# Routing of a two-layer trunk: expert loads held behind two row gathers, token table made before the gates

## What is computed

```python
x = x + concat([y_a, y_b, y_c]) @ w_out[l]
h2 = rmsnorm(x, norm2_g[l])
x = x + hier_moe(h2, ...)      # top-1 of 4 groups, top-2 of its 4 experts
# hier_moe
gate = one_hot(g_sel) * (p_g * w_e)
for gi in range(N_GROUPS):
    a = einsum('td,edh->teh', t, w_gate[gi]); b = einsum('td,edh->teh', t, w_up[gi])
    y = y + einsum('teh,ehd->td', silu(a) * b * gate[:, gi, :, None], w_down[gi])
```

## Time and profile before

| | us |
|---|---|
| median of 3 runs | 1200.66 (1200.47, 1200.66, 1204.75) |
| the profiled execution | 1201.01 |
| its span, first to last instruction | 1199.2 |
| PE busy in the span | 1143.3 (95%) |
| DVE, ACT busy | 999.9 (83%), 739.2 (62%) |
| granted TensorE clock, mean | 0.986 |

### The profile page before, as it was taken

How to read it: one execution, slowest core, us unless ns; L and a number is a source line. 1 busy time by engine, 2 the same in 40 slices (tenths; PEclk the granted TensorE clock), 3 DMA queues, 4 the chain that set the end, 5 groups by cost and what they waited for, 6 DMA issues and landing times.

```text
span 1199.2 us, 17704 instructions
## 1 busy us (share of the span) xinstructions
PE 1143.3 (95%) x5852; PEld 914.0 (76%) x5852; DVE 999.9 (83%) x1548; ACT 739.2 (62%) x1052; POOL 117.2 (10%) x156
## 2 busy tenths in 40 slices
PE   5999998999999999999889999989999999999995
PEld 4876885688788888888778668757887888888884
DVE  4997996447799999999769889863478999999997
ACT  5234238433688888888642341682337888888884
POOL 5100000001011111110400000000000111111022
PEclk9999999999999999999999999999989999999998
DMA  9722211128999999999864122012399999999987
GB/s 301 276 97 88 77 33 50 53 88 283 326 373 394 393 391 393 393 392 380 201 205 123 53 88 88 19 36 79 118 327 332 392 393 392 392 393 391 392 284 202
DMA packets 145564, 290.35 MB, mean 242 GB/s; under 512 B 17104, under 2 KB 19216, under 8 KB 145472
## 3 DMA queue, kind: packets, MB, share of 16 engines
q1 hardware_dynamic: 130176, 237.63, 55.5%
q0 software_dynamic: 15296, 51.56, 12.9%
HBM read 263.43 MB, written 25.69 MB: 241 GB/s over the span
## 4 chain that ended last, share of the span: by engine, by line
PE 67%; DVE 7%; ACT 3%; DMA 3%; issue 2%; POOL 2%; POOLq 0%; ACTq 0%; DVEq 0%
PE ps L387 19%; PE ps L389 18%; PE ps L388 18%; DVE w_lo L379 2%; PE ps L748 2%; PE ps L606 2%; DMA arena<-y_rows,yidx 2%; POOL x_sb L578 1%; PE ps L881 1%; PE ps L867 1%; PE ps L844 1%; PE ps L767 1%; PE ps L891 1%; DVE x_sb L1394 1%; DMA y_rows<-pw 1%
## 5 line engine op out<-in xcount | busy, mean ns | idle before, releaser
L387 PE MATMUL ps<-w_hi,a_hi 128*128 128x512 f32 x960 | 380.9, 397 | 5.7 <-DVE w_lo L379 4.8
L375 ACT ACTIVATE w_hi<-raw 128x1024 fp32r<-128x1024 f32 (+1 forms) x256 | 267.5, 1053 | 183.4 <-PE ps L389 173.2
L389 PE MATMUL ps<-w_hi,a_lo 128*128 128x512 f32 x960 | 375.0, 391 | 0.0
L388 PE MATMUL ps<-w_lo,a_hi 128*128 128x512 f32 x960 | 374.7, 390 | 0.0
L379 DVE TENSOR_TENSOR w_lo<-raw,w_hi 128x1024 fp32r<-128x1024 f32 (+1 forms) x256 | 302.2, 1209 | 52.3 <-ACT w_hi L375 44.0
L379 DVE TENSOR_TENSOR w_lo<-arena,w_hi 128x1024 fp32r<-128x1024 f32 x192 | 227.9, 1222 | 9.7 <-ACT w_hi L375 1.4
L375 ACT ACTIVATE w_hi<-arena 128x1024 fp32r<-128x1024 f32 x192 | 203.6, 1063 | 44.1 <-PE ps L389 39.1
L387 PEld LDWEIGHTS ps<-w_hi,a_hi 128*128 128x128 f32 x960 | 180.7, 188 | 43.9 <-issue 4.5
L389 PEld LDWEIGHTS ps<-w_hi,a_lo 128*128 128x128 f32 x960 | 180.6, 188 | 38.3
L388 PEld LDWEIGHTS ps<-w_lo,a_hi 128*128 128x128 f32 x960 | 180.9, 188 | 35.5
L387 PE MATMUL ps<-a_hi,w_hi 128*128 128x512 f32 (+1 forms) x304 | 121.4, 399 | 4.5 <-DVE a_lo L1418 3.1
(11 more groups left out here) (229 smaller groups left out, 1153.1 us busy)
## 6 DMA issues: line engine op xcount, KB each, us to landing
arena<-in_w_down SPq DMA_DIRECT2D x144, 256.0 KB
raw<-in_w_gate SPq DMA_DIRECT2D x136, 256.0 KB, 2.7
raw<-in_w_up SPq DMA_DIRECT2D x136, 256.0 KB, 2.9
arena<-in_w_gate SPq DMA_DIRECT2D x120, 256.0 KB
arena<-in_w_up SPq DMA_DIRECT2D x120, 256.0 KB
raw<-in_w_down SPq DMA_DIRECT2D x112, 256.0 KB, 9.1
raw<-in_w_in SPq DMA_DIRECT2D x80, 256.0 KB, 6.4
y_rows<-arena POOLq DMA_DIRECT2D x42, 256.0 KB, 5.9
```

Source lines behind the costliest of these rows:

```text
L375: nc.scalar.activation(split_slot(w_hi, n, w), place(S, i, n, w), ACT.Copy).then_inc(S.w_hi_set, 1)
L387: nc.tensor.matmul(o, lh, rh, start=start, stop=False)
L388: nc.tensor.matmul(o, lh, rl, start=False, stop=False)
L389: return nc.tensor.matmul(o, ll, rh, start=False, stop=stop)
```

## The change

Three things, in both layers.

SP waits, ahead of the second group, also for the landing of the gathers of experts 0 and 1.

The tables are made in two products. DVE writes the token half of `hot`, then the positions and `slots`, then the expert number `e2`, then copies `tab` and `count`; only then it computes the gates and the gate half of `hot`, which raises `hot_set` a ninth time. PE multiplies the token half (16 columns instead of 32), waits for the ninth `hot_set`, multiplies the gate half into another bank, and spins 8 times instead of 17. The copy to `gslot` has moved into `extras`, with a wait for the second product.

DVE makes the low part of expert piece 3 behind the split of the first tile, not ahead of it; and ACT waits for `ovx_set` earlier, ahead of its expert steps, at which point it has long been set.

```diff
--- before.py
+++ after.py
@@ -94,6 +94,7 @@
 C_SEL = C_PH + 32
 C_N = C_SEL + 20
 RW_COLS = 64
+HOT_SETS = 9
 HOTS, PRODUCTS, TABLES = 10, 11, 12
 HALF = SEQ // 2
 
@@ -452,6 +453,9 @@
 
                 sp.wait_ge(h2_stored, 16 * TT * (l + 1))
                 sp.wait_ge(ht_ready, 2 * DC * (l + 1))
+                for e in range(2):
+                    _, there, count = rows_of(main, l, None, e)
+                    sp.wait_ge(there, count)
                 for k in range(RAW + SIDE_MIX, RAW + SIDE_ROWS):
                     load_expert_piece(k)
                 for k in range(RING_E, RING_E + SPL):
@@ -724,10 +728,14 @@
                 mm.then_inc(pos_ready, 1)
                 spin(7, 4)
                 for q in range(TT * TOPE):
-                    pe.wait_ge(hot_set, TT * TOPE * l + q + 1)
-                    mm = T.matmul(ps[:, 3, 0:2 * E], slot_hot[:, q, :], R["hot"][:, q, :], start=(q == 0), stop=(q == TT * TOPE - 1))
+                    pe.wait_ge(hot_set, HOT_SETS * l + q + 1)
+                    mm = T.matmul(ps[:, 3, 0:E], slot_hot[:, q, :], R["hot"][:, q, 0:E], start=(q == 0), stop=(q == TT * TOPE - 1))
                 mm.then_inc(tab_ready, 1)
-                spin(7, 17)
+                pe.wait_ge(hot_set, HOT_SETS * (l + 1))
+                for q in range(TT * TOPE):
+                    mm = T.matmul(ps[:, 5, 0:E], slot_hot[:, q, :], R["hot"][:, q, E:2 * E], start=(q == 0), stop=(q == TT * TOPE - 1))
+                mm.then_inc(tab_ready, 1)
+                spin(7, 8)
                 pe.wait_ge(tab_set, 2 * (l + 1))
 
             def over_tables(l):
@@ -1258,6 +1266,7 @@
                     hi(sc, main, None, n + k)
                 tile_at(main, None, te)
                 n += 8
+                sc.wait_ge(ovx_set, l + 1)
 
                 def step(i, e):
                     m = n + e * PIECES_E
@@ -1283,7 +1292,6 @@
                 for e in range(E - 1):
                     step(None, e)
                 last_y(l, 0, n + PIECES_E * STORED + 8)
-                sc.wait_ge(ovx_set, l + 1)
                 extra = sc.value_load(ovx[0:1, EXTRA:EXTRA + 1], min_val=0, max_val=EXTRA)
 
                 def next_hi():
@@ -1515,28 +1523,34 @@
                                 ALU.add).then_inc(route_set, 1)
 
 
+                hot = R["hot"].rearrange("p (k t) n -> p k t n", k=TOPE)
+                V.tensor_tensor(hot[:, :, :, 0:E], R["m12"],
+                                cst[:, C_TOK:C_TOK + TT].unsqueeze(1).unsqueeze(3).to_broadcast(by_expert), ALU.mult)
+
+                ve.wait_ge(pos_ready, l + 1)
+                here = ps[:, 2, 0:TT * E].rearrange("p (t e) -> p t e", t=TT).unsqueeze(1).to_broadcast(by_expert)
+                link(V.tensor_tensor(R["tm"], here, R["m12"], ALU.mult))
+                link(V.tensor_reduce(R["p2"], R["tm"], AX, ALU.add))
+                slots()
                 link(V.tensor_tensor(R["tm"], cst[:, C_IOTA:C_IOTA + E].unsqueeze(1).unsqueeze(1).to_broadcast(by_expert),
                                      R["m12"], ALU.mult))
-                link(V.tensor_reduce(R["e2"], R["tm"], AX, ALU.add))
+                V.tensor_reduce(R["e2"], R["tm"], AX, ALU.add)
+                ve.wait_ge(tab_ready, 2 * l + 1)
+                V.tensor_copy(tab[:, 0:E], ps[:, 3, 0:E]).then_inc(tab_set, 1)
+                V.tensor_copy(R["count"], ps[:, 2, TT * E:(TT + 1) * E]).then_inc(tab_set, 1)
+
                 ve.wait_ge(exp_out, 2 * l + 2)
                 link(V.tensor_reduce(R["gs"], R["ge"], AX, ALU.add))
                 link(V.scalar_tensor_tensor(out=R["den"], in0=R["fe"], scalar=1.0, in1=R["gs"], op0=ALU.add, op1=ALU.mult))
                 link(V.reciprocal(gates[:, 0, :], R["den"]))
                 link(V.tensor_tensor(gates[:, 1, :], gates[:, 0, :], R["fe"], ALU.mult))
-                hot = R["hot"].rearrange("p (k t) n -> p k t n", k=TOPE)
-                V.tensor_tensor(hot[:, :, :, 0:E], R["m12"],
-                                cst[:, C_TOK:C_TOK + TT].unsqueeze(1).unsqueeze(3).to_broadcast(by_expert), ALU.mult)
-                link(V.tensor_tensor(hot[:, :, :, E:2 * E], R["m12"], gates[:].unsqueeze(3).to_broadcast(by_expert), ALU.mult))
-
-                ve.wait_ge(pos_ready, l + 1)
-                here = ps[:, 2, 0:TT * E].rearrange("p (t e) -> p t e", t=TT).unsqueeze(1).to_broadcast(by_expert)
-                link(V.tensor_tensor(R["tm"], here, R["m12"], ALU.mult))
-                link(V.tensor_reduce(R["p2"], R["tm"], AX, ALU.add))
-                slots()
-                ve.wait_ge(tab_ready, l + 1)
-                V.tensor_copy(tab[:, 0:E], ps[:, 3, 0:E]).then_inc(tab_set, 1)
-                V.tensor_copy(gslot[:, 0:E], ps[:, 3, E:2 * E])
-                V.tensor_copy(R["count"], ps[:, 2, TT * E:(TT + 1) * E]).then_inc(tab_set, 1)
+                V.tensor_tensor(hot[:, :, :, E:2 * E], R["m12"], gates[:].unsqueeze(3).to_broadcast(by_expert),
+                                ALU.mult).then_inc(hot_set, 1)
+
+            def slot_gates(l):
+
+                ve.wait_ge(tab_ready, 2 * l + 2)
+                V.tensor_copy(gslot[:, 0:E], ps[:, 5, 0:E])
 
             def slots(done=hot_set):
 
@@ -1553,6 +1567,7 @@
                     link(V.scalar_tensor_tensor(out=R["ex"], in0=R["count"], scalar=q, in1=R["ex"], op0=ALU.is_gt, op1=ALU.add))
                 V.scalar_tensor_tensor(out=R["b2"], in0=e2k[:], scalar=float(P), in1=p2k[:], op0=ALU.mult, op1=ALU.add)
                 V.tensor_scalar(R["c2"], e2k[:], float(STORED), None, ALU.is_lt)
+                slot_gates(l)
                 link(V.tensor_tensor_scan(R["cum"], cst[:, C_ONE:C_ONE + E], R["ex"], 0.0, ALU.mult, ALU.add))
                 link(V.scalar_tensor_tensor(out=R["c2"], in0=p2k[:], scalar=128.0, in1=R["c2"], op0=ALU.is_lt, op1=ALU.mult))
                 V.tensor_tensor(first_of[:], R["cum"], R["ex"], ALU.subtract)
@@ -1799,11 +1814,12 @@
                 norm_copy(2 * l + 1)
                 route(l)
                 extras(l)
-                for j in range(9, 12):
+                for j in range(9, 11):
                     lo(ve, main, None, n0 + PIECES_IN + j)
                 n = n0 + PIECES_MIX
                 te = E * l
                 tile_xt(main, None, te)
+                lo(ve, main, None, n0 + PIECES_IN + 11)
                 for k in range(4, 8):
                     lo(ve, main, None, n + k)
                 tile_mul(main, None, te)
```

## The result

| | before | after |
|---|---|---|
| median of 16 runs each, us | 1201.92 (1199.22 to 1204.75) | 1208.01 (1203.57 to 1211.28) |
| profiled execution and its span | 1201.01, 1199.2 | 1210.08, 1208.2 |
| its mean granted clock | 0.986 | 0.978 |
| mean clock over the runs | 0.9855 (30 runs, below) | 0.9796 (16 runs) |

The ratio is 1.0050, 95% interval 1.0038 to 1.0061: slower by 6 us, outside the range of the prediction. The profiled execution is 9.07 us above that of before, so it shows somewhat more than the typical loss.

The account below looks back on a forecast made before the run. PE is busy through the expert stage, so only its ends could move: start +0.4, clock at 315 0, end +0.5, sum +0.9 on 1201.01 gives 1201.9, median 1201.5; range 1198.5 to 1205.5 us.

Parts of the forecast that it names:

- The token table: Table product at the routing: tab copied at 291.3 in layer 0; gather issued 0.5 us earlier there, 0.7 in layer 1.
- The gather beside no loads: First expert's gather with the second group held: lands 4.0 us after issue, bounds 3.4 and 4.9.
- The gates' table: Second product before the first expert: PE idle 1.4 us, then 16 passes, 2.0 us at full clock or 3.4 at low.
- I take product at full clock, spins at the low one: Clock choice at both layer starts: layer 0 +0.8 us, layer 1 -0.4, sum +0.4.
- DVE is late: Layer 0 start at full clock: DVE's chain, not the gather, ends last, giving the expert's matmuls at 300.15 against 299.95.
- the low case: Both layer starts with everything at the low clock: +2.2 and +1.0, the outer end of +3.2 us.
- The clock at 315: Half-rate stretch 315 to 318.5 in layer 0, 1.7 us lost: change put at 0, ends -1.7 and +1.7.
- The held loads: Expert-stage loads queued behind SP's wait: some 3.5 us of DMA work carried to layer 1's end, costing +0.5 us.
- No wait on PE: Expert stages: the held loads make PE wait for no weights.
- 13 us to spare: End of layer 1: ACT splits the last piece at 1173.75, while DMA engines stand at 0.20 from 1160 on.
- the debt comes out at the end: Rival, chance 0.14: layer 1's last store and row gathers slowed, up to 4.8 us for the store; 1204 to 1210.
- quick gather, clock stays up: Rival, chance 0.16: start worth -0.8 us, clock at 315 perhaps -1.7; 1198.2 to 1199.9.

Follow-up runs that it names:

- the late product without a hold: Changed kernel without the hold, gates' product behind the first tile's transposes, 13 spins ahead of them, gslot copied later: 1207.34 us, ratio 1.0048.

## Why the prediction was wrong, step by step

**The token table**: right, 291.36 for 291.3. **The gather beside no loads**: right, 4.2 us for 4.0, in both layers. It was worth nothing because PE came to the transposes 3.6 us after the landing: the gather wasn't late, as the prediction had said, but by far more than it had.

**The gates' table**: this is the step that failed, in two places. The gap was 1.35 us for 1.4. But "I take product at full clock, spins at the low one", with the reason that "the fall probably comes later too", was wrong. In layer 0 the clock was down from 290.8, within the token table's product and ahead of the gap, and in layer 1 from 888.1, in the gap; before, it had fallen at 291.3 and 881.8. It stayed down through product and spins in both layers, and through the transposes. The product took 3.60 us, at the end that was called 3.4 for the low clock. And "DVE is late" was wrong: DVE idled 1.11 us for PE's transposes, and DVE's chain comes next at best, as the kernel without spins suggests. The start was sized at +0.8 - 0.4 = +0.4; it measured +2.8 + 1.6 = +4.4. That is above the outer end of +3.2, since the sum of the low case left the transposes at 2.64 us: from their start to the matmuls it was 3.11 and 3.33.

The low case was in the sum, but the choice between its ends had no row behind it. Rows 4 had the same place of layer 1 with 34 passes in 6.85 us, the low clock right behind a gap of 0.56; a longer gap gave no reason to expect less. With the low ends the sum would have been 1204.4 for the median, in the range, though still below the 1208. The start is the term that was most mis-sized, by 4.0 us.

**The clock at 315**, put at 0 with ends of 1.7 either way: in the profiled run the stretch was there once in layer 0, as before, and also in layer 1 (915.4), and two more came at 611.6 and 778.9. Over the runs the clock is 0.006 lower, 7.1 us of PE time; the two starts, half of (10.2 + 10.2 - 3.4 - 6.9), are 5.05 us of it. Whether the stretches far from the routing belong to the change isn't shown: the trace of the hold alone, which had the tables of before, has one too, from 772.9.

**The held loads.** "No wait on PE" and the last store's 2.29 us hold in the trace of after. But the step is wrong where it counts, as the hold alone shows, in two places. The debt was counted as the ten DMAs of the second group, 6.7 us less 3.2 for the hole from 904 on; the hole repaid what had been said (3.7 us), but 3.6 MB were missing ahead of it, 9.3 us, since the loads behind the group stand behind the same wait. And "13 us to spare" was measured to the split of the last piece, while the first of the six that count as landed together is split 7.3 us earlier; ACT waited 3.3 us. The hold costs 0.0016, about 1.9 us, for the +0.5 of the sum. The trace of the whole change shows no such wait; that the late expert and the low stretch at 915.4 give the loads time there is an argument and not shown. Whether the hold costs anything beside the tables is open: 1.0050 with it and 1.0036 without have overlapping intervals.

The rival *the debt comes out at the end* named a real mechanism and one of its two places: POOL waited 5.63 us for the store in the trace of the hold, and the store took 5.98 us in that of the longer one. ACT's weights, which it didn't name, end the chain of the hold alone. The rival *quick gather, clock stays up* had the clock the wrong way round.

Of the rule on turns between queues (the Trainium skill, DMA: Bandwidth & Descriptors, Queues, rings and completion order), the runs show more than the estimate from it: the gather lands 4.1 to 4.2 us after its issue beside no loads, and 4.9, 5.2, 5.7 and 5.7 us beside them (before in both layers, the late product without a hold, 13 spins alone), so loads cost it 0.7 to 1.6 us where the estimate was at most 1.3. A 256 KB store lost 3.7 us, against 0.7 us for its own bytes at 392 GB/s, so taking turns by itself doesn't account for it. The Trainium skill (TensorE: Matmul & The Clock Gate, A second HAM failure mode: psum-queue depth-cycling) also tells of a kernel of 512-column matmuls in which PE idled briefly between groups of matmuls often enough for its clock to go back and forth. The trace agrees in kind, for short matmuls: 0.50 for 10.2 us with PE busy for 8.85 of them and no idle time above 1.35 us.
